# One VectorE order changed inside the attention loop, one normalization moved to VectorE, and five TensorE waits dropped

## The chip, the cores and the metric

The kernel runs on one core of a Trainium2 chip. The metric is the device time of one execution in microseconds (us). The kernel before takes 1023.63 us, the median of 3 runs (1023.41 to 1023.95).

## What is computed

Two decoder layers over 512 tokens of width 1024, all in float32: a diagonal state-space layer with a gated output and a squared-ReLU MLP, then one layer of sliding-window attention (window 128, 16 query heads in groups of 4 over 4 key/value heads, one learned sink logit per head) with another MLP, and a final RMSNorm. The change lies in the attention:

```
q = (hn @ w_q + b_q)                      # 512 x 1024, 16 heads of 64
s = einsum(q, k) * scale                  # per block of 128 queries: 256 keys (previous and own block)
s = where(valid, s, -inf)
m = maximum(max(s), sink)
p = exp(s - m)
denom = sum(p) + exp(sink - m)
o = einsum(p / denom, v)
h = h + o @ w_o + b_o
```

## The kernel before, in words

Every engine has its own instruction stream, and they meet only through semaphores: an engine stops at a wait until the counter has reached a value, and what stands behind the wait on that engine stops with it. Large products are written as three TensorE products of split operands (high by high, high by low, low by high), each with 512 columns; `unit` issues one output tile of 128 x 512 as 8 k-tiles of three such matmuls (L1714 to L1716).

The attention runs over 16 "quads" Q. One quad is 4 heads of one block of 128 queries: `u = Q // 4` is the head group, `n = Q % 4` the block. For n = 0 there is no previous block, so such a quad has 128 keys for each head instead of 256, and all its instructions are half as long. The stages of a quad are:

1. `scores` (TensorE, L1922): 4 matmuls (8 records in the trace) into two banks of PSUM, from the query tiles `2u` and `2u+1` of `qT`.
2. `sinks` (VectorE, L1444) puts the sink logit beside the scores; `maxima` (VectorE) adds the mask (L1449, out of PSUM) and takes the negated maximum (L1455).
3. `exps` (ScalarE, L834): four exponentials with sums, one for each head.
4. `denominators` (VectorE, L1461): the reciprocal of the four sums.
5. `norm_p` (ScalarE, L841): four scalings of the probabilities by the reciprocals, in place in `s_sb`.
6. `turn_p` (TensorE, L1934): transposes of the probabilities into PSUM.
7. `turned`: one half copied to `pT` by ScalarE (L847), the other by VectorE (L1466).
8. `mix` (TensorE, L1947): the product with the values; it waits for both halves of `pT`.
9. `o_hi` (ScalarE, L853) and `o_low` (VectorE, L1472): the result as a high and a low part.

`skewed(stages)` issues them as a software pipeline: for each step 0, 1, 2, ... it calls every stage in the listed order with the quad `step - lag`. So the list is the order of the engine's instructions within a step. Before, the lists are:

```
TensorE: (scores, 0), (mix, 3), (turn_p, 2), (dense, None)
ScalarE: (norm_p, 1), (o_hi, 3), (turned, 2), (exps, 0), (next_pair, None)
VectorE: (sinks, 0), (denominators, 1), (maxima, 0), (next_queries, 1), (turned, 2), (o_low, 3), (next_pair, None)
```

`dense` fills TensorE between the small attention matmuls: in steps 0 to 10 it computes half a query tile (12 matmuls of 512 columns; tile 3 is complete at the end of step 2, tile 5 of step 6, tile 7 of step 10), in steps 11 to 15 a quarter of an output projection tile (6 matmuls), in steps 16 to 18 two or three quarters (12, 12 and 18). A finished query tile is scaled on VectorE by `queries(m)` (L1431, L1433): `next_queries` calls it for tiles 2 to 7 in steps 1, 3, 5, 7, 9 and 11, behind the maxima of that step. The scores of quads 4, 8 and 12 are the first that read the tiles 3, 5 and 7, and they are issued one step after these tiles' `queries`.

In step Q, TensorE's `scores(Q)` waits for its query tiles (`q_done`), for the previous quad's mask addition, which frees the score banks (`s_masked`), and for keys and values (`kv_done`). `turn_p` waits for the normalization of its quad (`p_norm`) and for both copies of the quad before (`pt_a`, `pt_v`), which `mix` of the same step has waited for already. Waits with a value of zero are left out, so the first quads have fewer.

Of the kernel before, what the change touches and what calls it, by code (L numbers as in the profile page):

```python
# [14 lines left out]
P = 128  # L15
D = 1024
L = 512
KT = D // P
# [19 lines left out]
DEEP = 3  # L38
NQ = 16
NKV = 4  # L40
BLK = 128
NBLK = L // BLK
QUADS = 4
LAM_MAX = -1e-4


MLP_OUT, MLP_LAST = HK, HK + N_OUT * HK
# [87 lines left out]
def build(nc, panels, pairs, xu_d, x_d, lam_d, turns_d, prm_d, dd_d, cst_d, mask_d, col_d, out_d):  # L135
    ctx = ExitStack()
    with ctx:
        def sb(name, shape, dt=F32, where=ctx):
            return where.enter_context(nc.sbuf_tensor(name, shape, dt))
# [106 lines left out]
        s_sb = sb("s_sb", [P, DEEP, 4, 2 * BLK + 1], where=over)  # L246
# [3 lines left out]
        rden = sb("rden", [P, DEEP, 4], where=over)  # L250
# [37 lines left out]
        kv_done = sem("kv_done")  # L288
        q_done, s_mm, s_masked, m_step = sem("q_done"), sem("s_mm"), sem("s_masked"), sem("m_step")
        p_exp, rden_done, p_norm = sem("p_exp"), sem("rden_done"), sem("p_norm")  # L290
        pt_mm, pt_v, pt_a = sem("pt_mm"), sem("pt_v"), sem("pt_a")
# [3 lines left out]
        def wait(eng, s, value):  # L295

            if not (isinstance(value, int) and value <= 0):
                eng.wait_ge(s, value)
# [32 lines left out]
        def window(n):  # L331

            return slice(BLK if n == 0 else 0, 2 * BLK)

        def halves_of(n):
            return (1,) if n == 0 else (0, 1)
# [216 lines left out]
        def _(a):  # L553
# [282 lines left out]

            def norm_p(Q):
                u, n, r = Q // NBLK, Q % NBLK, Q % DEEP
                a.wait_ge(rden_done, Q + 1)
                for j in range(4):  # L840
                    act_fn(s_sb[:, r, j, window(n)], s_sb[:, r, j, window(n)], ACT.Copy,  # L841
                           scale=rden[:, r, j:j + 1]).then_inc(p_norm, 1)
# [20 lines left out]
            for m in range(KT):  # L863
                u = U_SIDE + m
# [11 lines left out]
        def _(v):  # L876
            tt, ts, stt = nc.vector.tensor_tensor, nc.vector.tensor_scalar, nc.vector.scalar_tensor_tensor
            mul, add, sub = ALU.mult, ALU.add, ALU.subtract
# [549 lines left out]
            def queries(m):  # L1428

                v.wait_ge(unit_done, U_Q + 1 + m)  # L1430
                tt(t1[:], ps[:, query_bank(m), :], rstd[:], ALU.mult).then_inc(bank_free, 1)  # L1431
                v.wait_ge(bank_free, 4 + B_Q + 1 + m)
                ts(qT[:, m, :], t1[:], COLS("b_q")[:, m:m + 1], HD ** -0.5, ALU.add, ALU.mult).then_inc(q_done, 1)  # L1433
                v.wait_ge(q_done, m + 1)
# [23 lines left out]
            def denominators(Q):  # L1458
                u, n, r = Q // NBLK, Q % NBLK, Q % DEEP
                v.wait_ge(p_exp, 4 * Q + 4)  # L1460
                nc.vector.reciprocal(rden[:, r], den[:, r]).then_inc(rden_done, 1)  # L1461

            def turned(Q):
                u, n, q = Q // NBLK, Q % NBLK, Q % 2
                v.wait_ge(pt_mm, Q + 1)
                ts(pT[:, q, 2:4].rearrange("p t b n -> p t (b n)")[:, :, window(n)],  # L1466
                   ps[:, 5, :].rearrange("p (t m) -> p t m", t=2)[:, :, window(n)], 1.0, None, ALU.mult).then_inc(pt_v, 1)
# [6 lines left out]
                   hid[:, 0, 0, 2 * u:2 * u + 2, bass.ds(n * BLK, BLK)].bitcast(F32),  # L1474
                   ALU.subtract).then_inc(ot_lo, 1)

            def next_queries(Q):
                if Q % 2 == 0 and 2 + Q // 2 < KT:
                    queries(2 + Q // 2)

            def next_pair(Q):
                if Q == QUADS * NBLK:
# [6 lines left out]
                elif Q == QUADS * NBLK + 2:  # L1489
                    head_rest(PAIRS, FOURTH)  # L1490
                    head_rest(PAIRS, LAST)

            skewed([(sinks, 0), (denominators, 1), (maxima, 0), (next_queries, 1), (turned, 2), (o_low, 3),
                    (next_pair, None)])


            for m in range(KT):
# [3 lines left out]
                u = U_SIDE + m  # L1501
# [17 lines left out]
        def _(pe):  # L1519
# [392 lines left out]

            def scores(Q):
                u, n, q = Q // NBLK, Q % NBLK, Q % 2
                wait(pe, q_done, 2 * u + 2)
                wait(pe, s_masked, Q)
                wait(pe, kv_done, 2 + NBLK)
                at = window(n)
                for t in range(2):
                    for e in range(2):  # L1920
                        r = slice(64 * e, 64 * e + 64)
                        last = mm(ps[:, e, t * 2 * BLK + at.start:(t + 1) * 2 * BLK], qT[r, 2 * u + t, n * BLK:(n + 1) * BLK],  # L1922
                                  kT[r, u // 2, (n - 1) * BLK + at.start:(n + 1) * BLK], start=True, stop=True)
                last.then_inc(s_mm, 1)

            def turn_p(Q):
                u, n, r = Q // NBLK, Q % NBLK, Q % DEEP
                pe.wait_ge(p_norm, 4 * Q + 4)
                wait(pe, pt_a, Q)
                wait(pe, pt_v, Q)  # L1930
                for j in range(4):
                    for b in halves_of(n):
                        at = (j % 2) * 2 * BLK + b * BLK
                        last = turn(ps[:, 4 + j // 2, at:at + BLK], s_sb[:, r, j, b * BLK:(b + 1) * BLK], ident)  # L1934
                last.then_inc(pt_mm, 1)
# [45 lines left out]
def skewed(stages):  # L1981

    last = QUADS * NBLK
    longest = max(lag for _, lag in stages if lag is not None)
    for Q in range(last + longest):
        for stage, lag in stages:
            if lag is None:
                stage(Q)  # L1990
            elif 0 <= Q - lag < last:
                stage(Q - lag)
# [116 lines left out]
```

## Time and profile before

| | |
|---|---|
| median of 3 runs | 1023.63 us (1023.41 to 1023.95) |
| the profiled execution | 1024.0 us |
| its span | 1022.2 us, mean granted TensorE clock 0.994 |
| TensorE matmul busy | 996.6 us (97%) |
| VectorE busy | 822.5 us (80%) |
| ScalarE busy | 484.9 us (47%) |
| GpSimd busy | 274.5 us (27%) |
| attention steps 0 to 18 | about 552.8 to 648 us of the span |

The span runs from the first to the last instruction in the trace; the profiled execution's time is 1.8 us longer. In a timeline row the first number is the start, the second the length in us, and a bracket at the end tells how long the engine stood idle before it and what the profile takes for the releaser. Where a wait is for several semaphores, the profile names one of them. Overlapping matmuls are shown with modelled ends, so start times are the ones to compare.

### The profile page before, as it was taken

The numbers are of one execution on the slowest core, as the hardware profiler recorded it, in microseconds if no ns is written. First come the engines' busy times: TensorE is split into PE (matmuls) and PEld (weight loads), VectorE is DVE, ScalarE is ACT, GpSimd is POOL, SyncE is SP. The second block draws the span as 40 slices with busy tenths as digits, with TensorE's granted clock in tenths as the row PEclk, the third lists the DMA queues.
The fourth block names the chain that finished last, engine by engine and source line by source line (L and its number), as shares of the span: only waits on it lengthen the run. The fifth ranks groups of instructions, "written<-read, shape, count | busy, mean of one in ns | idle before, by whom it ended". The sixth has DMA issues, their size and how long they took to land.

```text
span 1022.2 us, 16652 instructions
## 1 busy us (share of the span) xinstructions
PE 996.6 (97%) x5850; PEld 821.8 (80%) x5850; DVE 822.5 (80%) x1155; ACT 484.9 (47%) x880; POOL 274.5 (27%) x232
## 2 busy tenths in 40 slices
PE   9789999999999999999999999999999999999996
PEld 4677888888888888888888776888888888888886
DVE  7994488698898988986895777889898898989845
ACT  7763323455354444543421878555455354444421
POOL 8995887400000000030967240010000000001150
PEclk9899999999999999999999999999999999999998
DMA  6124333222412223230333110232322412234012
GB/s 255 35 41 136 125 113 134 83 83 83 161 65 103 95 110 124 82 123 1 103 118 122 55 42 21 85 123 102 104 83 82 157 69 103 90 113 147 21 42 83
DMA packets 31877, 97.53 MB, mean 95 GB/s; under 512 B 10696, under 2 KB 13256, under 8 KB 27984
## 3 DMA queue, kind: packets, MB, share of 16 engines
q1 hardware_dynamic: 31824, 96.83, 27.4%
q8 instruction: 32, 0.52, 0.2%
q14 instruction: 21, 0.17, 0.1%
HBM read 92.36 MB, written 2.10 MB: 92 GB/s over the span
## 4 chain that ended last, share of the span: by engine, by line
PE 84%; DVE 6%; ACT 4%; issue 2%; SPq 1%; POOL 1%; DMA 1%; POOLq 0%; DVEq 0%; ACTq 0%
PE ps L1754 17%; PE ps L1757 9%; PE ps L1775 8%; PE ps L1776 8%; PE ps L1777 8%; PE ps L1714 6%; PE ps L1716 6%; PE ps L1715 6%; PE ps L1660 2%; PE ps L1662 2%; PE ps L1661 2%; DVE act L1076 2%; SPq L390 1%; PE ps L1947 1%; PE ps L1922 1%
## 5 line engine op out<-in xcount | busy, mean ns | idle before, releaser
L451 POOL TENSOR_TENSOR gate_sb<-gate_sb 128x1 f32<-128x1 f32 x52 | 18.4, 355 | 713.6 <-DMA raw<-panels_in 502.1
L1776 PE MATMUL ps<-hid,w_hi 128*128 128x512 f32 x384 | 150.5, 392 | 0.0
L1775 PE MATMUL ps<-hid,w_hi 128*128 128x512 f32 x384 | 150.4, 392 | 0.0
L1777 PE MATMUL ps<-hid,w_lo 128*128 128x512 f32 x384 | 149.6, 390 | 0.0
L703 ACT ACTIVATE s_hi<-w_raw 128x1024 fp32r<-128x1024 f32 (+1 forms) x104 | 87.8, 845 | 99.7 <-PE ps L1757 94.1
L540 POOL TENSOR_TENSOR w_lo<-raw,w_hi 128x1024 fp32r<-128x1024 f32 x52 | 130.2, 2505 | 4.3
L1754 PE MATMUL ps<-hid,s_hi 128*128 128x512 f32 x448 | 121.3, 392 | 0.7 <-ACT acc L767 0.7
L1714 PE MATMUL ps<-hid,w_hi 128*128 128x512 f32 x304 | 120.3, 396 | 0.0
L1715 PE MATMUL ps<-hid,w_hi 128*128 128x512 f32 x304 | 118.6, 390 | 0.0
L1716 PE MATMUL ps<-hid,w_lo 128*128 128x512 f32 x304 | 118.4, 390 | 0.0
L1186 DVE TENSOR_TENSOR s_lo<-w_raw,s_hi 128x1024 fp32r<-128x1024 f32 (+1 forms) x104 | 101.9, 990 | 17.7 <-ACT s_hi L703 10.1
L751 ACT ACTIVATE t<-t 128x512 f32<-128x512 f32 x56 | 35.4, 632 | 130.8 <-DVE t L1219 130.8
L1754 PEld LDWEIGHTS ps<-hid,s_hi 128*128 128x128 f32 x448 | 80.0, 188 | 14.7 <-ACT acc L767 1.1
L1754 PE MATMUL ps<-act,s_hi 128*128 128x512 f32 x336 | 90.7, 392 | 0.0
L1777 PEld LDWEIGHTS ps<-hid,w_lo 128*128 128x128 f32 x384 | 72.1, 188 | 15.7
L1775 PEld LDWEIGHTS ps<-hid,w_hi 128*128 128x128 f32 x384 | 72.4, 189 | 12.9
L1776 PEld LDWEIGHTS ps<-hid,w_hi 128*128 128x128 f32 x384 | 72.4, 188 | 12.0
L1757 PEld LDWEIGHTS ps<-hid,s_lo 128*128 128x128 f32 x448 | 68.6, 189 | 9.2
L1233 DVE TENSOR_TENSOR h<-ps,h 128x512 f32<-128x512 f32 x96 | 65.7, 685 | 9.2 <-PE ps L1777 9.1
L1757 PE MATMUL ps<-hid,s_lo 128*128 128x256 f32 x448 | 71.2, 281 | 0.0
L1754 PEld LDWEIGHTS ps<-act,s_hi 128*128 128x128 f32 x336 | 60.4, 188 | 10.5
L1716 PEld LDWEIGHTS ps<-hid,w_lo 128*128 128x128 f32 x304 | 57.1, 188 | 12.3
(274 smaller groups left out, 2043.9 us busy)
## 6 DMA issues: line engine op xcount, KB each, us to landing
raw<-panels_in SPq DMA_DIRECT2D x108, 512.0 KB, 3.3
w_raw<-pairs_in SPq DMA_DIRECT2D x28, 1024.0 KB, 5.5
xy<-xu_in SPq DMA_DIRECT2D x4, 512.0 KB, 7.5
out<-h SPq DMA_DIRECT2D x8, 256.0 KB, 2.1
prm<-prm_in SPq DMA_DIRECT2D x1, 1280.0 KB, 5.7
h<-x_rows_in SPq DMA_DIRECT2D x1, 1280.0 KB, 12.8
h<-x_rows_in SPq DMA_DIRECT2D x1, 768.0 KB, 7.0
dd<-dd_in SPq DMA_DIRECT2D x1, 256.0 KB, 5.7
```

The source lines that it names most:

```text
L540: nc.gpsimd.tensor_tensor(w_lo[:, s, :], raw[:, s % 2, :], w_hi[:, s, :].bitcast(F32), ALU.subtract).then_inc(w_split, 1)
L703: act_fn(s_hi[:, first:last + 1, :].rearrange("p b n -> p (b n)"), raw_blocks(blocks), ACT.Copy).then_inc(s_hi_done, 1)
L1186: tt(s_lo[:, first:last + 1, :].rearrange("p b n -> p (b n)"), raw_blocks(blocks), s_hi[:, first:last + 1, :].rearrange("p b n -> p (b n)" ...
L1233: tt(h[:, m, :], ps[:, (j + shift) % 4, :], h[:, m, :], ALU.add).then_inc(bank_free, 1)
L1714: mm(ps[:, bank, :], w_hi[:, s, w], x[:, 0, k, :], start=(k == 0), stop=False)
L1715: mm(ps[:, bank, :], w_hi[:, s, w], x[:, 1, k, :], start=False, stop=False)
L1716: last = mm(ps[:, bank, :], w_lo[:, s, w], x[:, 0, k, :], start=False, stop=(k == KT - 1))
L1754: mm(both, s_hi[:, b, w], x(k), start=(start and k == 0), stop=False, skip_group_check=True)
L1757: last = mm(to[:, main], s_lo[:, b, w], x(k)[:, 0], start=False, stop=(k == HK - 1), skip_group_check=True)
L1775: mm(to, w_hi[:, s, w], hid[:, 0, 0, HK * par + k, :], start=(k == 0), stop=False)
L1776: mm(to, w_hi[:, s, w], hid[:, 0, 1, HK * par + k, :], start=False, stop=False)
L1777: last = mm(to, w_lo[:, s, w], hid[:, 0, 0, HK * par + k, :], start=False, stop=(k == HK - 1))
```

## The change

Three edits, all in the attention:

1. VectorE's `next_queries` is split in two. The tiles 3, 5 and 7 (those that the next step's scores need) are scaled by `due_queries`, now first in steps 3, 7 and 11, ahead of the sinks, the reciprocal and the maxima; tiles 2, 4 and 6 stay behind the maxima as `later_queries`.
2. For the last head group (quads 12 to 15) the normalization is no longer four ScalarE activations but one VectorE multiplication of all four heads by the broadcast reciprocals, placed after the reciprocal and ahead of the maxima of the next quad.
3. TensorE's `scores` waits for `q_done` only at n = 0 and for `kv_done` only at Q = 0; `turn_p` no longer waits for `pt_a` and `pt_v`.

```
+BY_DVE = QUADS * NBLK - NBLK
...
 # ScalarE
             def norm_p(Q):
                 u, n, r = Q // NBLK, Q % NBLK, Q % DEEP
+                if Q >= BY_DVE:
+                    return
                 a.wait_ge(rden_done, Q + 1)
...
 # VectorE
+            def norm_p(Q):
+                u, n, r = Q // NBLK, Q % NBLK, Q % DEEP
+                if Q < BY_DVE:
+                    return
+                v.wait_ge(rden_done, Q + 1)
+                part = s_sb[:, r, :, window(n)]
+                tt(part, part, rden[:, r].unsqueeze(2).to_broadcast([P, 4, len(halves_of(n)) * BLK]), mul).then_inc(p_norm, 4)
...
-            def next_queries(Q):
-                if Q % 2 == 0 and 2 + Q // 2 < KT:
+            def next_queries(Q, due):
+                if Q % 2 == 0 and 2 + Q // 2 < KT and (Q % NBLK == NBLK - 2) == due:
                     queries(2 + Q // 2)
+
+            def due_queries(Q):
+                next_queries(Q, True)
+
+            def later_queries(Q):
+                next_queries(Q, False)
...
-            skewed([(sinks, 0), (denominators, 1), (maxima, 0), (next_queries, 1), (turned, 2), (o_low, 3),
-                    (next_pair, None)])
+            skewed([(due_queries, 1), (sinks, 0), (denominators, 1), (norm_p, 1), (maxima, 0), (later_queries, 1), (turned, 2),
+                    (o_low, 3), (next_pair, None)])
...
 # TensorE
             def scores(Q):
                 u, n, q = Q // NBLK, Q % NBLK, Q % 2
-                wait(pe, q_done, 2 * u + 2)
+                if n == 0:
+                    wait(pe, q_done, 2 * u + 2)
                 wait(pe, s_masked, Q)
-                wait(pe, kv_done, 2 + NBLK)
+                if Q == 0:
+                    wait(pe, kv_done, 2 + NBLK)
...
             def turn_p(Q):
                 u, n, r = Q // NBLK, Q % NBLK, Q % DEEP
                 pe.wait_ge(p_norm, 4 * Q + 4)
-                wait(pe, pt_a, Q)
-                wait(pe, pt_v, Q)
```

## Rows read from the trace of the kernel before

**Rows 1.** The page, parts 1 and 4: busy time by engine, and the ending chain
```profile
PE 996.6 (97%) x5850; PEld 821.8 (80%) x5850; DVE 822.5 (80%) x1155; ACT 484.9 (47%) x880; POOL 274.5 (27%) x232
...
PE 84%; DVE 6%; ACT 4%; issue 2%; SPq 1%; POOL 1%; DMA 1%; POOLq 0%; DVEq 0%; ACTq 0%
```

**Rows 2.** Waits in 552 to 644 us: line, releaser, us, times, longest
```profile
PE ps L1922 <- DVE qT L1433: 1.0, 2, 0.7
```

**Rows 3.** Windows: length, busy PE, PEld, DVE, ACT, POOL, granted clock, DMA share, GB/s
```profile
622.00:635.00 13.00, 11.94 (x77) 8.09 (x76) 8.64 (x17) 12.14 (x40) 0.00 (x0) 1.00 0.01 1
644.00:1010.00 366.00, 365.49 (x1868) 311.67 (x1867) 302.33 (x424) 165.85 (x245) 29.38 (x24) 1.00 0.27 94
```

**Rows 4.** Timeline of TensorE around the scores of quads 4 and 8
```profile
569.94 0.39 PE L1716 MATMUL ps<-hid,w_lo 128*128 128x512 f32 x1
571.48 0.87 PE L1947 MATMUL ps<-pT,v_sb 128*64 128x256 f32 x6
...
592.64 0.39 PE L1716 MATMUL ps<-hid,w_lo 128*128 128x512 f32 x1
592.96 0.71 PE L1922 MATMUL ps<-kT,qT 64*128 64x128 f32 x8
593.60 1.08 PE L1947 MATMUL ps<-pT,v_sb 128*64 128x256 f32 x8
```

**Rows 5.** Timeline of steps 10 to 12, TensorE and VectorE
```profile
609.34 0.39 PE L1716 MATMUL ps<-hid,w_lo 128*128 128x512 f32 x1
610.84 1.23 DVE L1449 TENSOR_TENSOR s_sb<-ps,mask 128x1024 f32<-128x1024 f32 x1 [0.59 <-PE ps L1922]
613.24 0.68 DVE L1431 TENSOR_TENSOR t<-ps,rstd 128x512 f32<-128x512 f32 x1
613.40 0.40 PE L1716 MATMUL ps<-hid,w_lo 128*128 128x512 f32 x1
614.48 0.69 DVE L1466 TENSOR_SCALAR pT<-ps 128x512 f32<-128x512 f32 x1
615.27 1.08 PE L1947 MATMUL ps<-pT,v_sb 128*64 128x256 f32 x8
```

**Rows 6.** Timeline of steps 14 to 16
```profile
627.10 0.51 ACT L834 ACTIVATE s_sb<-s_sb,negm 128x257 f32<-128x257 f32 x1
629.21 0.18 DVE L1461 RECIPROCAL rden<-den 128x4 f32<-128x4 f32 x1 [1.41 <-ACT s_sb L834]
629.31 1.19 DVE L1449 TENSOR_TENSOR s_sb<-ps,mask 128x1024 f32<-128x1024 f32 x1
630.54 1.23 DVE L1455 TENSOR_REDUCE negm<-s_sb 128x4 f32<-128x1028 f32 x1
631.68 0.68 DVE L1466 TENSOR_SCALAR pT<-ps 128x512 f32<-128x512 f32 x1
...
631.31 0.58 ACT L847 ACTIVATE pT<-ps 128x512 f32<-128x512 f32 x1
631.79 0.51 ACT L834 ACTIVATE s_sb<-s_sb,negm 128x257 f32<-128x257 f32 x1
...
632.46 1.08 PE L1947 MATMUL ps<-pT,v_sb 128*64 128x256 f32 x8 [1.06 <-ACT pT L847]
```

**Rows 7.** Timeline of VectorE behind the attention: SBUF to SBUF, 1024 and 512 columns
```profile
636.48 1.22 DVE L1116 TENSOR_TENSOR w_raw<-w_raw 128x1024 f32<-128x1024 f32 x1
637.72 0.69 DVE L1119 TENSOR_TENSOR w_raw<-w_raw 128x512 f32<-128x512 f32 x1
```

**Rows 8.** Timeline of TensorE: last two matmuls of a stage, first transpose
```profile
561.19 0.38 PE L1922 MATMUL ps<-kT,qT 64*128 64x256 f32 x2
561.50 0.66 PE L1934 MATMUL ps<-cst,s_sb 128*128 128x128 f32 x4
```

**Rows 9.** Timeline and windows (columns as in rows 3) early in the kernel
```profile
33.64 1.71 PE L1618 MATMUL ps<-toep,xy 128*64 128x128 f32 x16 [2.41 <-DMA toep<-k_even]
...
36.00:37.00 1.00, 1.00 (x24) 0.86 (x18) 1.00 (x2) 0.94 (x3) 1.00 (x2) 0.50 0.30 67
37.00:38.00 1.00, 1.00 (x15) 0.81 (x8) 0.97 (x3) 0.96 (x4) 1.00 (x1) 0.81 0.20 39
```

## The prediction

> **What bounds the kernel now.** I read the page first: TensorE is busy 97% of the span and holds 84% of the chain that ended last [rows 1]. So a change pays only where TensorE stands idle or does less, and this one leaves TensorE's work as it is. Next the waits: in the attention TensorE is idle 1.0 us in two waits of the scores for query tiles [rows 2], and 1.06 us in one wait of `mix` [rows 6]. Behind the attention it is busy 365.49 of 366 us [rows 3], so what the attention gains or loses reaches the end nearly whole. Last the timeline of the three places.
>
> The query waits are plain. Where nothing is late (quad 8), the short scores of an n = 0 quad start 0.32 us behind the last dense matmul (592.64, 592.96) and `mix` 0.64 us behind them [rows 4]. In step 4 the last dense matmul starts at 569.94, so `mix` could start at 570.90 and starts at 571.48: 0.58 us. In step 12 it is 613.40, so 614.36, and in fact 615.27 [rows 5]: 0.91 us. Both contain a second effect: VectorE's half of the `pT` copy stood behind `queries` as well.
>
> The third place decides. `mix` of quad 13 starts at 632.46, and the profile names ScalarE's copy as the releaser. That copy ended at 631.31 + 0.58 = 631.89, 0.57 us earlier. VectorE's copy of the other half ends at 631.68 + 0.68 = 632.36, 0.10 us before the start [rows 6]. I take VectorE as the releaser. What does VectorE stand in? Steps 12 to 15 hold only 6 dense matmuls each, and TensorE is no longer the slowest; a ring is: exponentials of quad Q on ScalarE, then on VectorE reciprocal(Q), mask(Q+1), maximum(Q+1), then the exponentials of Q+1. One turn goes from 627.10 to 631.79, 4.69 us, in pieces of 2.11 (to the reciprocal at 629.21), 0.10 (to the mask), 1.23 (to the maximum) and 1.25 us (to the next exponentials) [rows 6]. None has slack.
>
> **Edit 1, the due query tiles.** No instruction is added; two on VectorE move forward, 1.24 us together (613.24 to 614.48 [rows 5]). In step 3 they fall into VectorE's wait for the exponentials and delay nothing; TensorE gets its 0.58 us. Steps 7 and 11 look alike, and I work out 11, where the ring starts. Tile 7 is complete at 609.34 + 0.39 = 609.73. VectorE starts perhaps 0.10 us later (my estimate, from the 0.10 between copy and `mix` above) and is through at 611.07. Sinks and reciprocal of quad 10 come next, some 0.17 us to the mask, which starts at 611.24 instead of 610.84 [rows 5]: 0.40 us later against a TensorE that is itself 0.58 us earlier, net 0.18 us earlier. ScalarE bears the late reciprocal: its normalization 10 and copy 9 then end at about the time that maximum 11 is ready. Step 7's lateness vanishes, because in steps 8 to 10, with 12 dense matmuls each, VectorE waits for the scores (0.59 us even before mask 11). TensorE also gets its 0.91 us in step 12 and is 1.49 us ahead, but it can't keep that: `mix(13)` is freed by the ring, which began only 0.18 us earlier. Alone this edit gives -0.18 us. If the ring's start didn't move at all, it would be 0; if VectorE were free in time, -0.58.
>
> **Edit 2, normalizing quads 12 to 15 on VectorE.** ScalarE loses four activations a quad, which ran beside the ring. VectorE gets one instruction a quad, between reciprocal(Q) and mask(Q+1): into the ring. The old trace has no multiplication with this broadcast operand, but near ones: two float32 operands and the result in SBUF take 1.22 us for 1024 columns and 0.69 for 512 [rows 7]. The next instruction starts 0.09 us before such an end (630.54 + 1.23 against 631.68 [rows 6]), so VectorE is held for 1.14 or 0.61 us. The multiplication waits for the reciprocal right before it: its 0.18 and some 0.03 for the semaphore, 0.21 instead of the 0.10 that the mask needed. So a full quad adds 0.21 + 1.14 - 0.10 = 1.25 us to a turn, the short quad 12 adds 0.21 + 0.61 - 0.10 = 0.72. Ahead of mask(15), its maximum and the copy for `mix(13)` stand the normalizations 12, 13 and 14: 0.72 + 1.25 + 1.25 = 3.22 us. Bounds: an instruction that cost only its wait would give 3 x 0.11 = 0.3 us; three without overlap 0.8 + 1.35 + 1.35 = 3.5.
>
> Is some of it covered? ScalarE is no second ring any more: exponentials of 2.1 us and two copies (one 0.58 us) in a turn of 5.94. TensorE arrives at `mix(13)` at 631.40 in the old trace; it will now also wait before scores 15 (for mask 14) and `mix(12)`, but these waits are parts of the same delay and not added. Behind the ring's last turn its copy of quad 13 starts at 631.68 - 0.18 + 3.22 = 634.72, and `mix(13)` at 635.50 instead of 632.46. From there the others have air: normalization 15 ends near 634.83 + 2.11 + 0.21 + 1.22 = 638.4, and its transposes stand behind three stages of 1.0 us and 12 dense matmuls of 0.23, near 641.3. The 3.04 us stay to the end.
>
> **Edit 3, dropped waits.** `scores` loses one or two waits of three, `turn_p` two of three. The first `turn_p` has one wait already, since those of value zero are left out: it starts 0.31 us behind the last pair of the stage before [rows 8]. The scores of quad 8 with three waits start 0.32 us behind a dense matmul [rows 4]. A satisfied wait costs nothing that shows in starts, and I take 0. The other end: dense matmuls follow each other at 0.23 us, so 0.09 us at most at each boundary, at 10 scores and 9 transposes of steps 1 to 10, 1.7 us (those of steps 11 to 15 would be lost to the ring). A loss I exclude: nothing new is waited for.
>
> **Sum.** -0.18 + 3.22 + 0 = +3.04 us. The profiled execution took 1024.0, so its like would take 1027.0; that one lies 0.4 us above the median of the runs, and against the median it is 1023.63 + 3.04 = 1026.7 us.
>
> **The rivals.**
> A, the clock falls. TensorE's wait before `mix(13)` grows from 1.06 to about 3 us, with shorter ones shortly before. Early in the trace a gap of 2.41 us was followed by a stretch at 0.50, the 1.2 GHz level, until between 37 and 38 us [rows 9], some 3.4 us from the burst's start. At half speed 3.4 us lose 1.7: 1028.4. For: this gap would be longer. Against: around the early gap stood small matmuls, here dense ones, and 622 to 635 is at 1.00 in spite of its 1.06 us wait [rows 3].
> The Trainium skill ("TensorE: Matmul & The Clock Gate", section "HAM oscillation — how this bites in real kernels") tells the same mechanism: a long wait between bursts throttles TensorE, and the next burst starts at half clock. By that rule A is what this change brings; the trace agrees for the gap of 2.41 us.
> B, the chain is right and ScalarE frees `mix(13)`: its own ring of exponentials, normalization and two copies is as long. Relieved of the normalization it opens, and TensorE keeps everything: 0.58 + 0.91 + 1.06 = 2.55, 1021.1 us. For: the profile's name for the wait. Against: 0.57 us between that copy's end and the start, and the code, in which mask(Q+1) stands behind the multiplication. It needs the multiplications to delay the mask by under 0.06 us each.
> C, the dropped waits give their whole 1.7 us: 1025.0.
> D, the broadcast operand makes the multiplication half as long: 0.61 us less for two quads, 0.35 for the short one, 1.6 in all: 1025.1.
>
> **How the numbers follow.** Forecast 0.50; A 0.27; C and D together 0.14; B 0.05; several of B, C and D by halves, ending near no change, 0.04. The range 1025.0 to 1028.6 holds all but the last two. A measurement of this kernel can tell 0.2%, 2.05 us, from no change: slower begins at 1025.68. That is the forecast, A and some of C and D, 0.83; same is the rest of C and D and the mixed case, 0.12; faster is B, 0.05.
>
> **What would show it.** The new multiplication at 1.22 us x3 and 0.69 x1; a turn from exponentials 14 to 15 of 5.94 us; the query waits of scores 4 and 12 gone; a wait near 3 us before `mix(13)`; the distances on TensorE still 0.31. I am wrong if the turn stays under 5 us or that wait doesn't grow; if the clock in 630 to 645 is below 1.00, it is A.

## The result and the profile after

| | before | after |
|---|---|---|
| device time, median (range) of the runs made side by side, us | 1023.79 (1023.41 to 1025.68), 4 runs | 1032.44 (1031.08 to 1032.68), 4 runs |
| profiled execution: span, us | 1022.2 | 1030.9 |
| first scores to `mix(15)`, us | 89.23 | 98.55 |

The ratio is 1.008, 95% interval [1.0068, 1.0092]: slower by 8.7 us, where 3.0 were forecast and 1028.6 us was the upper end of the range. The direction was right, the size was not.

Most of this section is about the third line of the table, so first its rows. The start of the attention moves by some tenths between executions (552.06 to 554.61 us in those profiled here), so I measure from the first scores. TensorE of the kernel before, then of the kernel after (start us, length us, engine, line, operation, what it writes and reads):

```profile
552.84 0.71 PE L1922 MATMUL ps<-kT,qT 64*128 64x128 f32 x8
...
642.07 1.08 PE L1947 MATMUL ps<-pT,v_sb 128*64 128x256 f32 x8
```

```profile
552.29 0.71 PE L1941 MATMUL ps<-kT,qT 64*128 64x128 f32 x8
...
571.45 1.08 PE L1964 MATMUL ps<-pT,v_sb 128*64 128x256 f32 x8 [1.02 <-DVE pT L1477]
...
594.61 1.08 PE L1964 MATMUL ps<-pT,v_sb 128*64 128x256 f32 x8 [0.96 <-ACT pT L850]
...
615.97 0.71 PE L1941 MATMUL ps<-kT,qT 64*128 64x128 f32 x8 [1.16 <-DVE s_sb L1452]
617.78 1.08 PE L1964 MATMUL ps<-pT,v_sb 128*64 128x256 f32 x8 [1.09 <-ACT pT L850]
...
639.63 1.22 PE L1964 MATMUL ps<-pT,v_sb 128*64 128x256 f32 x8 [3.24 <-issue]
640.79 1.97 PE L1951 MATMUL ps<-cst,s_sb 128*128 128x128 f32 x8
...
646.02 1.08 PE L1964 MATMUL ps<-pT,v_sb 128*64 128x256 f32 x8
...
650.84 1.08 PE L1964 MATMUL ps<-pT,v_sb 128*64 128x256 f32 x8
```

Before, TensorE had two waits of the scores, 1.0 us together [rows 2], and one of `mix` [rows 6]. The wait of the scores of quad 4 is gone as intended. The scores of quad 12 no longer wait for their query tile but 1.16 us for the mask addition of quad 11, and waits of about 1 us stand before `mix(1)`, `mix(5)` and `mix(9)`. Why, VectorE's rows of step 11 tell, with GpSimd's of the same stretch behind them:

```profile
610.78 0.69 DVE L1434 TENSOR_TENSOR t<-ps,rstd 128x512 f32<-128x512 f32 x1 [1.18 <-PE ps L1733]
611.51 0.86 DVE L1436 TENSOR_SCALAR qT<-t,col 128x512 f32<-128x512 f32 x1
612.40 2.23 DVE L1447 TENSOR_SCALAR s_sb<-col 128x4 f32<-128x4 f32 x1
614.55 0.17 DVE L1464 RECIPROCAL rden<-den 128x4 f32<-128x4 f32 x1
614.63 1.19 DVE L1452 TENSOR_TENSOR s_sb<-ps,mask 128x1024 f32<-128x1024 f32 x1
```

```profile
610.89 0.19 POOL L452 TENSOR_TENSOR gate_sb<-gate_sb 128x1 f32<-128x1 f32 x1 [7.61 <-PE ps L1733]
611.05 1.04 POOL L538 TENSOR_SCALAR w_hi<-raw 128x1024 fp32r<-128x1024 f32 x1
612.17 2.43 POOL L541 TENSOR_TENSOR w_lo<-raw,w_hi 128x1024 fp32r<-128x1024 f32 x1
```

`sinks` writes four numbers a partition and takes 0.16 us in most steps. Here it takes 2.23 us and ends (614.63) with GpSimd's subtraction (614.60), which had started 0.23 us ahead of it. The query scaling in front of it takes 0.86 us instead of 0.49, beside GpSimd's other instruction. The meeting is no accident: the brackets show that VectorE's query scaling and GpSimd's split of the next weight panel are released by the same finished tile of TensorE (L1733), so what stands right behind a due query tile stands beside GpSimd's subtraction. Mask 11 stands 62.34 us behind the first scores, where it was 58.00 before (610.84 in [rows 5], less 552.84). The same pair of sinks and subtraction stands in steps 3 (566.02) and 7 (589.24). It had been in the old trace once, before the first quad, where I didn't look; VectorE, and GpSimd beside it:

```profile
552.05 2.22 DVE L1444 TENSOR_SCALAR s_sb<-col 128x4 f32<-128x4 f32 x1
```

```profile
551.82 2.43 POOL L540 TENSOR_TENSOR w_lo<-raw,w_hi 128x1024 fp32r<-128x1024 f32 x1
```

The last quad after (to be held against [rows 6]); VectorE:

```profile
635.03 0.18 DVE L1464 RECIPROCAL rden<-den 128x4 f32<-128x4 f32 x1 [1.40 <-ACT s_sb L835]
635.32 1.23 DVE L1472 TENSOR_TENSOR s_sb<-s_sb,rden 128x1024 f32<-128x1024 f32 x1
636.46 1.22 DVE L1452 TENSOR_TENSOR s_sb<-ps,mask 128x1024 f32<-128x1024 f32 x1
637.71 1.22 DVE L1458 TENSOR_REDUCE negm<-s_sb 128x4 f32<-128x1028 f32 x1
638.85 0.68 DVE L1477 TENSOR_SCALAR pT<-ps 128x512 f32<-128x512 f32 x1
```

and on ScalarE the first exponentials of quads 14 and 15, and between them the copy for `mix(13)`:

```profile
632.92 0.51 ACT L835 ACTIVATE s_sb<-s_sb,negm 128x257 f32<-128x257 f32 x1 [3.29 <-DVE negm L1458]
...
635.17 0.58 ACT L850 ACTIVATE pT<-ps 128x512 f32<-128x512 f32 x1
638.97 0.51 ACT L835 ACTIVATE s_sb<-s_sb,negm 128x257 f32<-128x257 f32 x1 [3.22 <-DVE negm L1458]
```

The ring is as forecast: the multiplication 1.23 us, one turn 6.05 us (forecast 5.94, before 4.69), the wait before `mix(13)` 3.24 us. For that wait the profile names no releaser. VectorE's half of the copy ends at 638.85 + 0.68 = 639.53, 0.10 us before the start; ScalarE's had ended at 635.75. Last the clock, the third column from the end (stretch, length, busy PE, PEld, DVE, ACT, POOL, clock, DMA share, GB/s):

```profile
635.00:640.00 5.00, 1.76 (x10) 1.13 (x11) 4.69 (x6) 1.78 (x8) 0.00 (x0) 1.00 0.00 0
640.00:642.00 2.00, 2.00 (x14) 1.44 (x11) 0.81 (x2) 1.32 (x6) 0.00 (x0) 0.61 0.00 0
642.00:644.00 2.00, 2.00 (x8) 1.71 (x7) 1.80 (x4) 1.21 (x2) 0.00 (x0) 0.53 0.00 0
644.00:1018.00 374.00, 373.55 (x1910) 317.07 (x1909) 307.67 (x431) 169.99 (x252) 29.30 (x24) 1.00 0.26 92
```

Behind the wait TensorE runs at the 1.2 GHz level for three to four microseconds: the transposes of quad 14 take 1.97 us instead of 1.09, and from `mix(13)` to `mix(14)` it is 6.39 us where it was 4.79 (before: 632.46 in [rows 6] to 637.25). That is rival A, 1.60 us. From 644 us on TensorE is busy 373.55 of 374 us, as before [rows 3]; what the attention lost is lost at the end.

### The profile page after: what moved, and what is told of

It reads as the page before. It is cut to its first block, busy times and chain, and to the rows that moved or that the text cites. A ratio compares the mean times of both kernels' runs of the same rounds, so it can differ in the third digit from the quotient of the medians.

```text
span 1030.9 us, 16614 instructions
## 1 busy us (share of the span) xinstructions
PE 998.3 (97%) x5850; PEld 823.0 (80%) x5850; DVE 834.6 (81%) x1159; ACT 478.5 (46%) x864; POOL 274.7 (27%) x232
## 4 chain that ended last, share of the span: by engine, by line
PE 81%; DVE 11%; issue 4%; ACT 2%; POOL 1%; POOLq 0%; DVEq 0%; ACTq 0%
PE ps L1771 16%; PE ps L1774 8%; PE ps L1792 8%; PE ps L1793 8%; PE ps L1794 8%; PE ps L1731 6%; PE ps L1732 6%; PE ps L1733 6%; PE ps L1677 2%; PE ps L1678 2%; PE ps L1679 2%; DVE act L1079 2%; PE ps L1964 1%; PE ps L1951 1%; ACT s_sb L835 1%
## 5 line engine op out<-in xcount | busy, mean ns | idle before, releaser
L1733 PE MATMUL ps<-hid,w_lo 128*128 128x512 f32 x304 | 118.7, 390 | 0.0
L1733 PEld LDWEIGHTS ps<-hid,w_lo 128*128 128x128 f32 x304 | 57.2, 188 | 12.3
```

The costliest lines, as they stand in the source:

```text
L1733: last = mm(ps[:, bank, :], w_lo[:, s, w], x[:, 0, k, :], start=False, stop=(k == KT - 1))
```

## The experiments

Unless said otherwise each is the kernel before with the edit shown, timed beside it on one chip in groups (medians of the kernel before: 1023.51 us beside e1 to e4, 1023.2 beside both e5, e6 and e8, 1023.46 beside e7, e9 and e10, 1023.21 beside e11 and e12). In the code, `...` marks lines left out. The table first, since it carries the argument: how much later than before each stage of TensorE starts, counted from the first scores of each trace, in us.

| kernel | time, median | `mix(1)` | `mix(5)` | `mix(9)` | `mix(12)` | `mix(13)` | `mix(14)` | `mix(15)` |
|---|---|---|---|---|---|---|---|---|
| the change | 1032.44 | +0.52 | +1.56 | +3.06 | +5.54 | +7.72 | +9.32 | +9.32 |
| e1, waits alone | 1023.14 | 0.00 | +0.01 | +0.01 | 0.00 | +0.01 | +0.03 | +0.03 |
| e2, query tiles alone | 1027.79 | +0.52 | +1.57 | +3.06 | +3.36 | +4.19 | +4.20 | +4.20 |
| e3, normalization alone | 1028.1 | 0.00 | 0.00 | +0.01 | +1.25 | +3.43 | +5.05 | +5.05 |
| e4, query tiles behind sinks | 1023.33 | -0.57 | -0.55 | -1.19 | -0.88 | -0.05 | -0.04 | -0.03 |
| e5, sinks by reduce | 1024.18 | -0.57 | -0.55 | -1.12 | -0.82 | +0.01 | +1.64 | +1.64 |
| e5, sinks by tensor_tensor | 1029.3 | +0.52 | +1.55 | +3.05 | +3.36 | +4.18 | +4.19 | +4.19 |
| e6, normalization off the ring | 1025.85 | 0.00 | -0.01 | 0.00 | +0.30 | +1.13 | +2.74 | +2.74 |
| e7, the change, sinks first | 1028.82 | -0.57 | -0.56 | -1.19 | +1.28 | +3.46 | +5.11 | +5.07 |
| e8, e3 and matmuls in the wait | 1026.53 | 0.00 | 0.00 | +0.05 | +1.29 | +3.47 | +3.49 | +3.50 |
| e9, orders turned round | 1022.35 | 0.00 | +0.02 | -0.61 | -0.52 | -1.29 | -0.92 | -0.92 |
| e10, e4 and matmuls in the wait | 1023.27 | -0.57 | -0.56 | -1.14 | -0.84 | -0.01 | -0.02 | -0.02 |
| e11, e6 and matmuls in the wait | 1025.15 | 0.00 | 0.00 | +0.05 | +0.39 | +1.22 | +1.24 | +1.24 |
| e12, e9, waits, 14 and 15 on VectorE | 1022.16 | 0.00 | +0.02 | -0.62 | -0.52 | -1.29 | -1.22 | -1.22 |

Read down a column to see what an edit costs there, and along a row to see where it arises. The three edits tried one by one add up to the change: 0.03 + 4.20 + 5.05 = 9.28 against 9.32.

**e1, the dropped waits alone.**
```diff
-                wait(pe, q_done, 2 * u + 2)
+                if n == 0:
+                    wait(pe, q_done, 2 * u + 2)
...
-                wait(pe, kv_done, 2 + NBLK)
+                if Q == 0:
+                    wait(pe, kv_done, 2 + NBLK)
...
-                wait(pe, pt_a, Q)
-                wait(pe, pt_v, Q)
```


> Only edit 3: the waits on q_done, kv_done, pt_a and pt_v are dropped, nothing else. Theory (port): satisfied waits are free, 0.0 us (within 0.5 us of the kernel before), and the starts on TensorE keep their 0.31 us from stage to stage. Rival (queue): each dropped wait gives up to 0.09 us, 1.0 to 1.7 us faster, with distances of 0.22 to 0.25.


Measured: ratio 0.9997 [0.9988, 1.0006], no stage moved by more than 0.03 us. Dropping a wait that is satisfied long before is worth nothing here.

**e2, the due query tiles alone.**
```diff
-            skewed([(sinks, 0), (denominators, 1), (maxima, 0), (next_queries, 1), (turned, 2), (o_low, 3),
...
+            skewed([(due_queries, 1), (sinks, 0), (denominators, 1), (maxima, 0), (later_queries, 1), (turned, 2),
...
```


> Only edit 1: the due query tiles are scaled first in steps 3, 7 and 11, ahead of the sinks. Theory (port): TensorE's finished query tile releases VectorE's queries and GpSimd's weight split at the same time; the sinks, a float32 multiplication of VectorE from SBUF to SBUF, then fall onto GpSimd's subtraction of 2.4 us and last 2.2 us instead of 0.16 in each of the three steps; mask 11 comes some 4 us later, the ring carries it, TensorE's clock stays at 1.00 before mix 13 or falls once: 1027.5 to 1029.5 us. Rival (the prediction's sum): the move costs nothing, 1023.6.


Measured: ratio 1.0042 [1.0028, 1.0056]. The sinks take 2.23 us in steps 3, 7 and 11. The waits for query tiles that the edit removes come back larger, and the longest, 1.9 us, stands before `mix(13)` (waiting line, releaser, us in all, times, longest):
```profile
PE ps L1953 <- ACT pT L847: 4.0, 3, 1.9
PE ps L1928 <- issue: 1.1, 1, 1.1
PE ps L1953 <- DVE pT L1466: 1.0, 1, 1.0
```

**e3, the normalization alone.**
```diff
+BY_DVE = QUADS * NBLK - NBLK
... in ScalarE's norm_p:
+                if Q >= BY_DVE:
+                    return
... and VectorE's norm_p as in the change; then VectorE's list, cut behind the maxima:
-            skewed([(sinks, 0), (denominators, 1), (maxima, 0),
+            skewed([(sinks, 0), (denominators, 1), (norm_p, 1), (maxima, 0),
```


> Only edit 2: the last quad group is normalized on VectorE ahead of the maxima. Theory (ring): each full quad adds 1.25 us to the turn, 0.7 for the short one, TensorE's wait before mix 13 grows by 3.2 to 3.4 us: 1027.0 us, and 1.6 more where the clock falls to 0.50 behind that wait (1028.6). Rival (all of the loss is edit 1): 1023.8 to 1024.5. The sinks stay at 0.16 us in every step but the first.


Measured: ratio 1.0042 [1.0029, 1.0056]. `mix(13)` is 3.43 us late, `mix(14)` 5.05: the two parts, the ring (forecast 3.22) and the clock (1.62), stand apart in the table. TensorE's rows:
```profile
635.33 1.54 PE L1964 MATMUL ps<-pT,v_sb 128*64 128x256 f32 x8 [3.24 <-issue]
636.80 1.97 PE L1951 MATMUL ps<-cst,s_sb 128*128 128x128 f32 x8
```

**e4, the query tiles early, but behind the sinks.** Against e2 (the rest of the list, cut here, is the same):
```diff
-            skewed([(due_queries, 1), (sinks, 0), (denominators, 1),
+            skewed([(sinks, 0), (due_queries, 1), (denominators, 1),
```


> Edit 1 with one difference: the sinks of steps 3, 7 and 11 are issued ahead of the due query tiles. Theory (port): the sinks run before GpSimd starts and take 0.16 us; the second instruction of queries may still be drawn out from 0.49 to 0.86 us; the time is that of the kernel before, 1023.2 to 1024.2. Rival (placement: whatever stands behind queries is held for 2 us, by VectorE's wait for its own result): the reciprocal or the mask behind it is held now, 1027.5 or more.


Measured: ratio 1.0 [0.9991, 1.0009]. This is what the forecast had thought edit 1 to be. TensorE runs up to 1.19 us ahead and gives it back before `mix(13)`, where its wait is 1.9 us. With the sinks over before GpSimd starts, mask 11 comes at 610.26, 58.09 us behind the first scores (before 58.00).

**e5, what holds the sinks?** Both have the edit of e2, with the sinks in front of GpSimd's subtraction as there, and another instruction for them.
```diff
-ts(s_sb[:, r, :, 2 * BLK:], sink.unsqueeze(2), 1.0, None, ALU.mult).then_inc(m_step, 1)
+nc.vector.tensor_reduce(s_sb[:, r, :, 2 * BLK], sink.unsqueeze(2), AX.X, ALU.max).then_inc(m_step, 1)
```


> The due query tiles go first in their steps, ahead of the sinks, as in the run that had this move alone (1027.79 us, sinks of steps 3, 7 and 11 at 2.23 us behind GpSimd's 2.43 us subtraction). The only difference: the sinks are written by tensor_reduce (max over one element) instead of tensor_scalar. Theory P (what holds the sinks is an access to SBUF that VectorE's two-element mode and GpSimd's instruction take from each other; the Trainium skill, SBUF — State Buffer, section Who interferes with whom, has it that a tensor_reduce never contends): the sinks last 0.2 us in all 16 steps, mask(11) comes at about 610.4, and the time is 1023.3 to 1024.3 us. Theory Q (any small instruction of VectorE on SBUF that stands behind the query tile stays behind GpSimd's instruction, or it waits for a semaphore that the trace does not show): 2.2 us in steps 3, 7 and 11 again, 1027.3 to 1028.3 us.


```diff
-ts(s_sb[:, r, :, 2 * BLK:], sink.unsqueeze(2), 1.0, None, ALU.mult).then_inc(m_step, 1)
+tt(s_sb[:, r, :, 2 * BLK:], sink.unsqueeze(2), sink.unsqueeze(2), ALU.max).then_inc(m_step, 1)
```


> The same order (due query tiles ahead of the sinks), and the sinks written by tensor_tensor max of the sink column with itself, two operands from SBUF. Theory P, with the rule of the Trainium skill, SBUF — State Buffer, section Who interferes with whom (an instruction of VectorE with two SBUF inputs contends with a GpSimd instruction that reads SBUF): the sinks of steps 3, 7 and 11 last 2.2 us again, 1027.3 to 1028.3 us. If only the two-element mode of tensor_scalar contends (theory P narrowed: a tensor_tensor on float32 does not take that mode), 0.2 us in all steps and 1023.3 to 1024.3 us. What the query tile's own scaling by tensor_tensor (0.69 us for 128x512, from PSUM and SBUF, beside GpSimd's work in the run of the move alone) shows speaks a little for the second.


Measured with the reduce: ratio 1.0005 [0.9996, 1.0014]; VectorE and GpSimd in step 11:
```profile
609.16 0.86 DVE L1433 TENSOR_SCALAR qT<-t,col 128x512 f32<-128x512 f32 x1
610.05 0.16 DVE L1444 TENSOR_REDUCE s_sb<-col 128x4 f32<-128x4 f32 x1
610.13 0.17 DVE L1461 RECIPROCAL rden<-den 128x4 f32<-128x4 f32 x1
610.21 1.20 DVE L1449 TENSOR_TENSOR s_sb<-ps,mask 128x1024 f32<-128x1024 f32 x1
```
```profile
609.83 2.44 POOL L540 TENSOR_TENSOR w_lo<-raw,w_hi 128x1024 fp32r<-128x1024 f32 x1
```
Measured with tensor_tensor: ratio 1.0056 [1.0043, 1.007]. The median, 1029.3, is above the range I gave, with runs from 1027.47 to 1030.56; the profiled one is the 1027.47, and its columns in the table are those of e2. The same places:
```profile
612.23 2.22 DVE L1444 TENSOR_TENSOR s_sb<-col 128x4 f32<-128x4 f32 x1
614.37 0.16 DVE L1461 RECIPROCAL rden<-den 128x4 f32<-128x4 f32 x1
```
```profile
612.00 2.43 POOL L540 TENSOR_TENSOR w_lo<-raw,w_hi 128x1024 fp32r<-128x1024 f32 x1
```
So it is not the place on VectorE, nor a semaphore that the place brings with it: at the same place the reduce starts and ends inside GpSimd's instruction, while tensor_scalar and a tensor_tensor with both operands from SBUF wait for its end. The mask addition (one operand from PSUM, one from SBUF) isn't held either: 1.20 us beside the same instruction. I had leaned to the narrower reading, in which a float32 tensor_tensor escapes; that is refuted. The Trainium skill ("SBUF — State Buffer", section "Who interferes with whom") has such a rule: VectorE shares one of its two pairs of SBUF ports with GpSimd, whoever issues first holds the pair for its whole instruction, tensor_scalar contends in its two-port modes and an instruction with two SBUF inputs contends with a GpSimd instruction that reads SBUF, and a tensor_reduce never does. The 2.23, 2.22 and 0.16 us agree. That the sinks' tensor_scalar ran in such a mode no trace shows. And no run takes GpSimd's subtraction away: that it is what holds the sinks rests on the ends of the two, which agree within 0.03 us each time, and on the kinds of instruction that are held.

That the reduce version's `mix(14)` stands at +1.64 has another cause: its wait before `mix(13)` is 1.9 us as in e4, but in this execution the clock fell behind it (0.50 in 632 to 634 us), and in those of e4 and e2 it didn't.

**e6, the same normalization behind the maxima.** Against e3:
```diff
-            skewed([(sinks, 0), (denominators, 1), (norm_p, 1), (maxima, 0),
+            skewed([(sinks, 0), (denominators, 1), (maxima, 0), (norm_p, 1),
```


> The last quad's normalization on VectorE, as in the run that had it alone (1028.1 us), but placed behind the maxima of its step instead of ahead of the mask: mask(Q) and max(Q) no longer stand behind norm(Q-1), and pT(Q-2) still does. Theory R (the loss is norm's 1.1 to 1.2 us in each turn of the ring exps, reciprocal, norm, mask, max, exps of quads 12 to 15, and what the clock takes after the long wait it makes): the ring turns in about 4.8 us as before, exps(15) starts near 1.3 us after mask(15) with mask(15) near 628.5 to 629.5, the wait before mix(13) is 1.1 to 2.4 us (norm(14) is now ahead of pT(13) on VectorE, +1.2), the clock stays at 1.00, and the time is 1023.0 to 1024.8 us. Theory S (what costs is that the probabilities are there later for TensorE, whatever the place): each of quads 12 to 14 has its turn later by 1 to 2 us and the time stays over 1026.5 us.


Measured: ratio 1.0017 [1.0007, 1.0026]; the median is above the range I gave, because I had taken the clock to stay. The wait before `mix(13)` is 1.89 us and the clock falls behind it, to 0.50. The place itself costs 1.13 us at `mix(13)` (3.43 in the ring).

**e8, TensorE kept busy in the wait of e3.** Seven matmuls whose result nothing reads go into the unused half of a PSUM bank. Against e3:
```diff
+                wait(pe, ot_lo, Q - 1)
+                if Q == BY_DVE + 1:
+                    for _ in range(7):
+                        mm(ps[:, 6 + q, 256:512], kT[:, 0, 0:128], kT[:, 0, 0:256], start=True, stop=True)
                 pe.wait_ge(pt_a, Q + 1)
                 pe.wait_ge(pt_v, Q + 1)
-                wait(pe, ot_lo, Q - 1)
```


> The last quad's normalization on VectorE, exactly as in the run that had it alone (1028.1 us; TensorE waits 3.24 us before mix(13), and the next 3.4 us of its work run at a granted clock of 0.50 to 0.69), and seven matmuls more (128x128 by 128x256, float32, about 0.4 us each, 3.0 us in all) into the unused half of mix(13)'s bank, in that wait; nothing reads them. Theory K (the wait itself costs 3.0 us, and the clock that falls after it 1.6 to 1.7 us more): with TensorE busy in the wait the clock stays at 1.00, mix(13) takes 1.0 us and the transposes 1.0 us, and the time is 1026.2 to 1026.9 us. Rival (the clock falls for another reason, or ScalarE and VectorE set the end, so that TensorE's pace after the wait is not on the path): 1027.8 to 1028.5 us. If the seven matmuls outlast the wait, the excess is added in both cases (at most 0.3 us).


Measured: ratio 1.0033 [1.0021, 1.0045]; the attention is 1.55 us shorter than e3's (5.05 less 3.50). The clock stays; the two columns `mix(13)` and `mix(14)` are now equal (+3.47, +3.49):
```profile
632.00:636.00 4.00, 3.78 (x22) 2.85 (x20) 3.34 (x5) 1.52 (x7) 0.00 (x0) 1.00 0.00 0
636.00:640.00 4.00, 4.00 (x24) 3.00 (x20) 3.30 (x5) 2.37 (x6) 0.00 (x0) 1.00 0.00 0
```
So more matmuls make e3's kernel faster, and the 1.6 us are the clock's alone. The Trainium skill ("TensorE: Matmul & The Clock Gate", section "HAM oscillation — how this bites in real kernels") has the mechanism: behind a long wait of TensorE the next burst of matmuls starts at the low clock. The traces agree; but the waits in its example are longer than the 1.89 us after which the clock fell in e6 and in e5's reduce, and here the measurement decides.

**e7, the whole change with the sinks first.** The edit is that of e4 on the kernel after.


> The whole change with one swap: the sinks stand ahead of the due query tile, so that they end before GpSimd's subtraction begins. Theory (losses add: 4.3 us are the sinks' 2.23 us behind GpSimd in steps 3, 7 and 11 with the waits of TensorE they make, 4.6 us the norm in the ring with the clock after it, and the dropped waits nothing): sinks 0.16 us in all steps but the first, mask(11) at about 610.3, the wait before mix(13) 3.2 us or a little more and then a granted clock near 0.5, and 1027.6 to 1028.4 us. Rival (the two losses overlap, so that taking one away from the whole change brings less than its price alone): over 1029.5 us.


Measured: ratio 1.0053 [1.0039, 1.0066], 0.4 us above the range. In the trace the whole loss is e3's (+5.07 against +5.05), and 4.25 us of the change's 9.32 are gone. So the rest of the change, without what the sinks lose, already stands at 1028.82, 0.2 us above the upper end of the prediction's range.

**e10, matmuls in the wait of e4.** Four instead of seven.


> The kernel with the due query tile behind the sinks (1023.33 us, 11 runs from 1022.81 to 1024.76; TensorE waits 1.9 us before mix(13)), and four matmuls more (128x128 by 128x256, float32, 0.38 us each, 1.5 us in all) in that wait, whose result nothing reads. After a wait of this length the clock stayed at 1.00 in one profiled execution and fell to 0.50 in two others (the sinks by tensor_reduce, and the norm behind the maxima). Theory K (the scatter of 1.5 to 2 us between executions of one kernel is this clock, which falls in some and not in others): the clock stays, and nearly all runs lie within 0.4 us of the lowest, median 1022.9 to 1023.2. Rival (the scatter comes from elsewhere in the kernel): as many runs 1 to 2 us above the lowest as before, median 1023.2 to 1023.6.


Measured: ratio 1.0 [0.9989, 1.001], runs from 1023.01 to 1027.84. (With e2 and e5's tensor_tensor there are three traces, not one, in which the clock stayed behind such a wait.) Here it stayed in the profiled execution too, but the scatter between runs stayed too, so the record is with the rival: most of it isn't from this wait. Two more traces show that some of it arises ahead of the attention: in the profiled executions of e11 (1026.82, its highest) and e12 (1023.64) the attention began at 554.61 and 553.89 instead of about 552.3. In e11 one early wait of TensorE for ScalarE (tile `v_ri`) is 3.1 us, where e2's trace has 1.1. The clock of the first 100 us doesn't tell the late starts from the others: it is 0.93 in e11 and 0.91 in e12, and also 0.93 in e2 and in e5's reduce, which began at 552.51 and 552.06.

**e11, e6 with four matmuls in the wait.** They are issued as in e8.


> The last quad's normalization on VectorE behind the maxima (1025.85 us; from the first scores to mix(15) 91.97 us where the kernel before has 89.23; TensorE waited 1.89 us before mix(13), and then the clock was 0.50), and four matmuls more (128x128 by 128x256, 0.38 us each, 1.5 us in all) in that wait, whose result nothing reads. Theory (of the 2.74 us, 1.6 to 1.8 are the clock, and only 1.0 the later place of the normalization, because off the ring it delays TensorE's transposes once and not in each turn): the clock stays at 1.00, first scores to mix(15) 90.0 to 90.5 us, time 1023.8 to 1024.5 us. Rival (the place itself costs more than 2 us, and the clock's part is the smaller): 91.2 to 92.0 us, and over 1025 us.


Measured: ratio 1.0014 [1.0005, 1.0023]; the median of 1025.15 is above the range and doesn't decide, the distances do: first scores to `mix(15)` 90.47 us, in the middle of what the theory gave. Of e6's 2.74 us 1.50 were the clock and 1.24 the place.

**e9, a version meant to beat both.** On the kernel before. The normalization stays on ScalarE; the mask and the maxima no longer stand behind the reciprocal.
```diff
-            skewed([(sinks, 0), (denominators, 1), (maxima, 0), (next_queries, 1), (turned, 2), (o_low, 3),
+            skewed([(sinks, 0), (next_queries, 1), (maxima, 0), (denominators, 1), (turned, 2), (o_low, 3),
... on VectorE, and on ScalarE:
-            skewed([(norm_p, 1), (o_hi, 3), (turned, 2), (exps, 0), (next_pair, None)])
+            skewed([(o_hi, 3), (turned, 2), (norm_p, 1), (exps, 0), (next_pair, None)])
```


> A version meant to beat both: the kernel before, with VectorE's order in a step sinks, query tile, mask and maxima, reciprocal, pT, O's low half, and ScalarE's order O's high half, pT, normalization, exps. Nothing else is changed; the last quad's normalization stays on ScalarE. The mask and the maxima of quad Q then need the scores alone, and are done while ScalarE still takes the exponentials of quad Q-1, so that the ring exps, reciprocal, mask, max, exps is cut: what remains is ScalarE's own work in a step (pT 0.6, O 0.4, norm 1.7, exps 2.1 us: 4.8 less overlaps). By a replay of the measured durations in this order TensorE's waits are 0.35 us before mix(13) and 0.46 before the transposes of quad 14 instead of 1.06 and more, and the end comes 1.7 us earlier: 1021.5 us, range 1021.0 to 1022.3. Rival 1 (ScalarE's pT ahead of norm makes TensorE's transposes late, or the reciprocal behind the maxima holds the normalization): 1023 to 1024.5 us. Rival 2 (a query tile ahead of the mask falls behind GpSimd's two instructions, which draws out more than its 0.37 us): +0.5 us a step in 3, 7 and 11, 1022.5 to 1023.5 us.


Measured: 1022.35 (1022.13 to 1023.51, 11 runs), ratio 0.9986 [0.9977, 0.9995]: faster than both kernels, by 1.1 us against the median beside it and 0.92 us in the trace, where 1.7 were expected; the time is just outside my range. All six query scalings take 0.86 us beside GpSimd, 0.37 more than in the kernel before, which is rival 2's ground. Rival 1 came about at one place: with the reciprocal behind the maxima the normalization of quad 0 starts late, and TensorE waits 0.52 us before the first transposes, where it had no wait before. It is 0.52 of the 0.78 us that are missing, if it reaches the end, which no run shows (`mix(1)` stands at 0.00 here and at -0.57 in e4). ScalarE and TensorE there:
```profile
560.22 1.28 ACT L841 ACTIVATE s_sb<-s_sb,rden 128x128 f32<-128x128 f32 x4 [3.47 <-DVE rden L1461]
561.54 0.66 PE L1934 MATMUL ps<-cst,s_sb 128*128 128x128 f32 x4 [0.52 <-ACT s_sb L841]
```
TensorE's waits left in the attention:
```profile
PE ps L1934 <- ACT s_sb L841: 0.8, 2, 0.5
PE ps L1947 <- ACT pT L847: 0.3, 1, 0.3
PE ps L1947 <- issue: 0.2, 1, 0.2
```

**e12, the change's three edits in such an order.** On the kernel after; `BY_DVE` is 14 here.
```diff
-            skewed([(due_queries, 1), (sinks, 0), (denominators, 1), (norm_p, 1), (maxima, 0), (later_queries, 1), (turned, 2),
+            skewed([(sinks, 0), (due_queries, 1), (later_queries, 1), (maxima, 0), (denominators, 1), (turned, 2), (norm_p, 1),
...
```
and ScalarE's order is that of e9.


> The edits of the change in an order that has neither of their two losses: the orders of the version of 1022.35 us (VectorE: sinks, query tile, mask and maxima, reciprocal, pT; ScalarE: O's high half, pT, normalization, exps), the waits dropped, and the normalization of quads 14 and 15 alone on VectorE, behind pT. With the ring cut, VectorE has time there (it waited 3.09 us before the reciprocal of quad 14 in that version), while ScalarE was on the path (norm 1.7 us, 0.28 us of TensorE's wait before the transposes of quad 14). By the replay of the measured durations TensorE's wait before the transposes of quad 14 goes, which gives 0.3 us: first scores to mix(15) 88.0 us (88.31 there), 1021.7 to 1022.4 us. Rival (the normalization on VectorE costs wherever it stands in the last quad, since 1.2 us are added to VectorE's step): 89 us or more, 1023 us or more.


Measured: 1022.16 (1021.89 to 1024.59, 11 runs) where the kernel before had 1023.21, ratio 0.9994 [0.9985, 1.0003]; first scores to `mix(15)` 88.01 us. By the times it can't be told from the kernel before, nor from e9; by the trace the attention is 0.3 us shorter than e9's, as forecast. The multiplication, here for quads 14 and 15 only and outside the ring, costs nothing; for quads 12 to 14 inside the ring it had cost 3.43 us and 1.62 more by the clock (e3):
```profile
630.23 1.22 DVE L1458 TENSOR_REDUCE negm<-s_sb 128x4 f32<-128x1028 f32 x1
631.37 0.17 DVE L1464 RECIPROCAL rden<-den 128x4 f32<-128x4 f32 x1
631.46 0.66 DVE L1477 TENSOR_SCALAR pT<-ps 128x512 f32<-128x512 f32 x1
632.03 1.22 DVE L1472 TENSOR_TENSOR s_sb<-s_sb,rden 128x1024 f32<-128x1024 f32 x1
```

## Why the prediction was wrong, step by step

- **What bounds the kernel.** Right. The wait before `mix(13)` hangs on VectorE's ring and not on ScalarE's copy, which the profile named: in e3 ScalarE has less to do and `mix(13)` comes 3.43 us later. And what TensorE gains ahead of the ring is lost there: e4 put it 1.2 us ahead, and at `mix(13)` -0.05 was left.
- **Edit 1, -0.18 us. This is the step that failed.** It said that the two instructions "fall into VectorE's wait for the exponentials and delay nothing", and that in step 11 "Sinks and reciprocal of quad 10 come next, some 0.17 us to the mask". In fact +4.20 us (e2). VectorE and GpSimd were taken as independent, as the text ahead of the prediction has it, where engines meet only through semaphores: the move puts the sinks behind the start of GpSimd's subtraction, beside which they last 2.07 us longer in each of three steps (e5 against e2). In step 3 this cost 0.52 us, up to step 7 1.57, up to `mix(9)` 3.06; the sentence that "Step 7's lateness vanishes" failed too, because TensorE itself had by then been made to wait. The ring, whose mask 11 comes 4.3 us later in the change, brought it to 4.19. Had the sinks stood first, the step's argument would nearly have held: e4 gives -0.03 instead of -0.18, and its mask 11 comes 0.27 us later than worked out, behind a query scaling drawn out by 0.37. The row that shows the conflict was in the old trace (552.05, 2.22 us), under a median of 0.16 us.
- **Edit 2, +3.22 us.** Right in mechanism and nearly in size: +3.43 at `mix(13)` (e3). From the reciprocal to the multiplication it took 0.28 to 0.29 us instead of the 0.21 worked out, three times. "The 3.04 us stay to the end" held for the delay of `mix(13)`, but not alone.
- **Edit 3, 0.** Right: e1, 0.03 us. Rivals B, C and D are refuted: ScalarE doesn't free `mix(13)` (`mix(13)` would not be late in e3), the waits give nothing, and the multiplication takes its 1.23 us.
- **Rival A came about besides**, with 1.60 us in the change, 1.62 in e3 and nothing in e8 with TensorE busy; the forecast 1.7. I gave it 0.27 on the ground that a 1.06 us wait had left the clock alone and that dense matmuls stand around this one, and the sum had no term for it. With the forecast's own growth of that wait to 3 us, beyond the 2.41 us of the early gap [rows 9], it deserved more.
- **Sum.** Forecast -0.18 + 3.22 + 0 = +3.04. Measured in the traces +4.20 + 3.43 + 1.62 + 0.03 = 9.28; the change has 9.32, less 0.55 us that its attention happened to start earlier: 8.8, and the spans differ by 8.7.

## What to carry to other kernels

When an instruction of VectorE moves, look at what GpSimd runs at the new place of it and of each one behind it, and not only at the free time on VectorE; the maximum of a group of equal instructions, far above its median, shows such a conflict before it is paid for. Work goes to an engine with spare time only if it stands outside the ring that sets the pace: the same multiplication cost 3.4 us inside, 1.2 behind the maxima, and nothing for the last two quads once the ring was cut. A forecast that makes a wait of TensorE grow to 3 us should count the lower clock behind it.

## What the runs showed of the hardware

- A VectorE instruction of four elements a partition, SBUF to SBUF, took 2.23 us as tensor_scalar (e2) and 2.22 as tensor_tensor (e5) beside GpSimd's 2.43 us subtraction, and 0.16 us as tensor_reduce at the same place (e5). So its price there is what is left of GpSimd's instruction, however small it is itself.
- The clock fell to the 1.2 GHz level after waits of TensorE of 3.24 us (three traces of three: the change, e3, e7). After waits of 1.9 us it fell in two traces (e6, e5's reduce) and stayed in three (e2, e4, e5's tensor_tensor). From `mix(13)` to `mix(14)` it cost 1.60 to 1.65 us each time, and matmuls in the wait gave back 1.50 (e11) and 1.55 us (e8). What decides after a wait of 1.9 us stays open.
